# Strassen-like weight sums of three feed-forward blocks made by accumulating on-chip transfers instead of by VectorE

## The reference

```python
def swiglu(x, w_gate, w_up, w_down):
    return (jax.nn.silu(x @ w_gate) * (x @ w_up)) @ w_down
# x = x + 0.5 * swiglu(rmsnorm(x, ffn_norm), w_gate, w_up, w_down), d_model 1024, d_ff 2816
```

## Time and profile before

| | us |
|---|---|
| median of 3 runs | 2056.55 (2053.38 to 2057.03) |
| span of the profiled execution | 2054.6 |
| TensorE busy in it | 2022.2 (98%) |
| VectorE busy | 1300.4 (63%) |
| ScalarE busy | 842.5 (41%) |
| GpSimd busy | 157.6 (8%) |

### The profile page before, as it was taken

The page is one execution under the profiler, slowest core; times in us unless marked ns, Lnnn a source line. Parts: engine busy times, 40 slices in busy tenths (PEclk is TensorE's granted clock), DMA queues, the critical chain, the costliest instruction groups (busy, mean ns, idle before and its releaser), DMA issues.

```text
span 2054.6 us, 44573 instructions
## 1 busy us (share of the span) xinstructions
PE 2022.2 (98%) x18982; PEld 1924.4 (94%) x18982; DVE 1300.4 (63%) x1821; ACT 842.5 (41%) x1310; POOL 157.6 (8%) x270
## 2 busy tenths in 40 slices
PE   8999999999999999999999999999999999999999
PEld 7999999997999999999999999998566799999998
DVE  5445476778348848566785775754774438657474
ACT  5222223263334525344452442544664335435252
POOL 3002002033000000000000000000036200000000
PEclk9999999999999999999999999999999999999999
DMA  7333233201252223231423232232146632322322
GB/s 149 90 98 85 77 92 108 78 12 26 74 153 84 83 83 124 92 97 60 134 95 116 90 107 77 85 102 59 42 130 164 176 104 83 124 83 89 117 73 73
DMA packets 243917, 194.45 MB, mean 95 GB/s; under 512 B 37668, under 2 KB 221874, under 8 KB 243730
## 3 DMA queue, kind: packets, MB, share of 16 engines
q1 hardware_dynamic: 235760, 180.51, 29.2%
q0 software_dynamic: 6256, 9.23, 1.6%
q10 hardware_dynamic: 1714, 2.02, 0.4%
HBM read 184.77 MB, written 3.02 MB: 91 GB/s over the span
## 4 chain that ended last, share of the span: by engine, by line
PE 88%; DVE 6%; ACT 3%; issue 2%; DMA 0%; ACTq 0%; SPq 0%; DVEq 0%
PE ps L2382 25%; PE ps L2311 25%; PE ps L2410 24%; PE ps L2324 3%; PE ps L2824 1%; PE ps L2930 1%; PE ps L2963 1%; PE ps L3086 1%; PE ps L2724 1%; DVE stmp L657 1%; PE ps L2694 1%; PE ps L3135 1%; PE ps L3100 1%; PE ps L2907 1%; DVE xl L1551 1%
## 5 line engine op out<-in xcount | busy, mean ns | idle before, releaser
L2311 PE MATMUL ps<-xh,wh 128*128 128x260 f32 x1120 | 295.4, 285 | 2.1 <-DVE xl L1551 1.4
L2311 PE MATMUL ps<-xl,wh 128*128 128x260 f32 x1120 | 292.0, 283 | 0.0
L2410 PE MATMUL ps<-xoh,wh 128*128 128x260 f32 x992 | 281.3, 284 | 1.3 <-DVE sq L1767 1.3
L2410 PE MATMUL ps<-xoh,wl 128*128 128x260 f32 x992 | 281.0, 283 | 0.0
L2410 PE MATMUL ps<-xol,wh 128*128 128x260 f32 x992 | 280.6, 283 | 0.0
L2382 PE MATMUL ps<-xh,wh 128*128 128x260 f32 x872 | 228.8, 284 | 0.7 <-DVE wl L1600 0.7
L983 ACT ACTIVATE wh<-rw 128x1024 fp32r<-128x1024 f32 (+1 forms) x135 | 138.8, 1029 | 218.9 <-PE ps L2382 152.0
L2382 PE MATMUL ps<-xl,wh 128*128 128x260 f32 x872 | 226.9, 282 | 0.0
L2311 PE MATMUL ps<-xh,wl 128*128 128x260 f32 x1120 | 225.8, 283 | 0.0
L906 ACT ACTIVATE wh<-raw 128x1024 fp32r<-128x1024 f32 (+1 forms) x90 | 100.5, 1116 | 294.2 <-PE ps L2311 285.9
L2311 PEld LDWEIGHTS ps<-xh,wh 128*128 128x128 f32 x1120 | 211.7, 189 | 7.1 <-issue 3.9
(11 more groups left out here) (546 smaller groups left out, 4363.3 us busy)
## 6 DMA issues: line engine op xcount, KB each, us to landing
rw<-ffn_w_gate SPq DMA_DIRECT2D x33, 1024.0 KB, 5.4
rw<-ffn_w_up SPq DMA_DIRECT2D x33, 1024.0 KB, 8.3
rw<-ffn_w_down SPq DMA_DIRECT2D x12, 2048.0 KB, 7.8
raw<-ffn_w_gate SPq DMA_DIRECT2D x22, 512.0 KB, 3.9
raw<-ffn_w_up SPq DMA_DIRECT2D x22, 512.0 KB, 3.9
raw<-ffn_w_down SPq DMA_DIRECT2D x16, 704.0 KB, 4.7
rw<-ffn_w_down SPq DMA_DIRECT2D x6, 1536.0 KB, 6.6
cb<-cache_ckv SPq DMA_DIRECT2D x72, 128.0 KB, 3.9
```

Source lines behind the costliest of these rows:

```text
L2311: got = mm(ps[0:width, bank + half, 0:HALF], w[par_][:, k * width:k * width + width], src[:, k0 + k, half * HALF:half * HALF + HALF], star ...
L2410: got = mm(ps[:, bank + mat, T0], w[:, cols], src[:, j, k, :], start=first and k == 0 and m == 0 and s == 0, stop=k == 3 and m == 1, skip_ ...
```

## The change

The four sums leave VectorE's list, with `ahead` and `begins`. GpSimd gets `sums_of_weights(name)`, called once for each of the three blocks. A sum is now made of transfers between places in SBUF, one for gate and one for up each time: a plain copy of one quarter into the buffer, and once that has landed, a transfer that adds the other quarter (`accum_op=ALU.add`). The buffers no longer swap: `one` holds the first sum, `two` the second and then the fourth, which is added in place once the second has been split. Two semaphores count the landings: `m_first` (first and third sums) and `m_second` (second and fourth). ScalarE waits for these instead of `z_sum`.

```diff
-                if kind[0] == "sum" and kind[2] in (1, 2, 4, 5):
-                    act.wait_ge(z_sum, Z["sum"] + 4 * rounds(kind[1]) + {1: 1, 2: 2, 4: 3, 5: 4}[kind[2]])
+                if kind[0] == "sum" and kind[2] == 1:
+                    act.wait_ge(m_first, M_FIRST + 96 * summed(name, kind[1]) + 64)
+                elif kind[0] == "sum" and kind[2] in (2, 5):
+                    act.wait_ge(m_second, M_SECOND + 96 * summed(name, kind[1]) + (64 if kind[2] == 2 else 96))
+                elif kind[0] == "sum" and kind[2] == 4:
+                    act.wait_ge(m_first, M_FIRST + 96 * summed(name, kind[1]) + 96)
...
-                def first_sum(p):
-
-                    load_ = sv.load[sv.start[p]]
-                    dve.wait_ge(z_in[load_ % 2], Z["in"][load_ % 2] + sv.landed(load_))
-                    if rounds(p) > 0:
-                        dve.wait_ge(z_sum, Z["sum"] + 4 * rounds(p))
-                    tt(sum_buf(name, p, 0), quarter(name, p, 0, 1), quarter(name, p, 4, 1), ALU.add).then_inc(z_sum, 1)
...
-                        ahead(n0 + 3)
...
-                        fourth_sum(p)
...
+                def split(p, j):
+
+                    pool.wait_ge(z_lo, Z["lo"] + sv.start[p] + j + 1)
+
+                def first(p):
+
+                    load_ = sv.load[sv.start[p]]
+                    pool.wait_ge(z_in[load_ % 2], Z["in"][load_ % 2] + sv.landed(load_))
+                    if rounds(p) > 0:
+                        split(p - 1, 1)
+                    else:
+                        pool.wait_ge(z_lo, Z["lo"] + sv.start[p] - 2)
+                    if summed(name, p) > 0:
+                        pool.wait_ge(m_first, M_FIRST + 96 * summed(name, p))
+                    for mat in range(2):
+                        pool.dma_start(one[:, mat], quarter(name, p, 0, 1)[:, mat]).then_inc(m_first, 16)
+                    pool.wait_ge(m_first, M_FIRST + 96 * summed(name, p) + 32)
+                    for mat in range(2):
+                        pool.dma_start(one[:, mat], quarter(name, p, 4, 1)[:, mat], accum_op=ALU.add).then_inc(m_first, 16)
+
+                def second(p):
+
+                    if rounds(p) > 0:
+                        split(p - 1, 5)
+                    for mat in range(2):
+                        pool.dma_start(two[:, mat], quarter(name, p, 0, 0)[:, mat]).then_inc(m_second, 16)
+                    pool.wait_ge(m_first, M_FIRST + 96 * summed(name, p) + 64)
+                    pool.wait_ge(m_second, M_SECOND + 96 * summed(name, p) + 32)
+                    for mat in range(2):
+                        pool.dma_start(two[:, mat], one[:, mat], accum_op=ALU.add).then_inc(m_second, 16)
+
+                def third(p):
+
+                    for mat in range(2):
+                        pool.dma_start(quarter(name, p, 0, 1)[:, mat], quarter(name, p, 0, 0)[:, mat], accum_op=ALU.add).then_inc(m_first, 16)
+
+                def fourth(p):
+
+                    split(p, 2)
+                    pool.wait_ge(m_second, M_SECOND + 96 * summed(name, p) + 64)
+                    for mat in range(2):
+                        pool.dma_start(two[:, mat], quarter(name, p, 4, 0)[:, mat], accum_op=ALU.add).then_inc(m_second, 16)
+
+                first(PLAIN)
+                second(PLAIN)
+                third(PLAIN)
+                for p in range(PLAIN, NF // 2):
+                    fourth(p)
+                    if p + 1 < NF // 2:
+                        first(p + 1)
+                        second(p + 1)
+                        third(p + 1)
```

More of the change, by code:

```diff
@@ L242, in counts @@
                 "xh": 7, "xl": 7, "xf": 5, "ev": 4 * PLAIN, "ps": 2 * PLAIN, "ph": 2 * PLAIN, "hh": NF // 2, "hl": NF,
-                "sum": 4 * r, "add": 4 * r, "seed": 2 * r, "p5": 2 * r, "u2": 2 * r, "sg": 3 * r, "h": 3 * r}
+                "add": 4 * r, "seed": 2 * r, "p5": 2 * r, "u2": 2 * r, "sg": 3 * r, "h": 3 * r}
 class Chain:
@@ L438, in yoco_step @@
         s_kb = [sem("s5_taps_blocks0"), sem("s5_taps_blocks1")]
+        m_first, m_second = g_in, gf_in
+        M_FIRST, M_SECOND = 240, 16
+        SUMS_BEFORE = {"ffn01": 0, "ffn10": TOGETHER, "ffn11": 2 * TOGETHER}
         y_tr, y_sb, y_out = sem("y_tr"), sem("y_sb"), sem("y_out")
@@ L442, in yoco_step @@
         z_hi, z_lo, z_used, z_up, z_xh, z_xl, z_xf = s_u, s_z, s_w, s_y1, s_yp, s_ysp, s_ct
-        z_ev, z_ps, z_ph, z_hh, z_hl, z_sum, z_add = s_ls, s_bb, s_bp, s_sn, s_tp, s_e, s_xe
+        z_ev, z_ps, z_ph, z_hh, z_hl, z_add = s_ls, s_bb, s_bp, s_sn, s_tp, s_xe
         z_seed, z_p5, z_u2, z_sg, z_h = s_ctc, s_sb, s_wb, s_x, s_sc
-        now = {"hi": 8, "lo": 2, "used": 4, "up": 1, "xh": 8, "xl": 1, "xf": 10, "ev": 1, "ps": 1, "ph": 1, "hh": 1, "hl": 8, "sum": 11,
+        now = {"hi": 8, "lo": 2, "used": 4, "up": 1, "xh": 8, "xl": 1, "xf": 10, "ev": 1, "ps": 1, "ph": 1, "hh": 1, "hl": 8,
                "add": 8, "seed": 8, "p5": 3, "u2": 16, "sg": 16, "h": 8, "in": (IN_0, IN_0)}
@@ L501, in raw_of, with sum_buf @@
             if j in (1, 2, 5):
-                return sum_buf(name, p, {1: 0, 2: 1, 5: 0}[j])
+                return sum_buf(name, {1: 0, 2: 1, 5: 1}[j])
             k0, m0 = {0: (0, 0), 3: (4, 0), 4: (0, 1), 6: (4, 1)}[j]
             return pair[:, :, k0:k0 + 4, m0 * P:m0 * P + P]
-        def sum_buf(name, p, which):
-            return sums_at[name][(p + which) % 2].rearrange("p (a k m) -> p a k m", a=2, k=4)
+        def sum_buf(name, which):
+            return sums_at[name][which].rearrange("p (a k m) -> p a k m", a=2, k=4)
         def quarter(name, p, k0, m0):
@@ L526, in rounds, with summed @@
             return p - PLAIN
+        def summed(name, p):
+            return SUMS_BEFORE[name] + rounds(p)
         def gbuf(p):
@@ L1604, in seven @@
                 sv, Z = SEV[name], ZB[name]
-                def first_sum(p):
-                    load_ = sv.load[sv.start[p]]
-                    dve.wait_ge(z_in[load_ % 2], Z["in"][load_ % 2] + sv.landed(load_))
-                    if rounds(p) > 0:
-                        dve.wait_ge(z_sum, Z["sum"] + 4 * rounds(p))
-                    tt(sum_buf(name, p, 0), quarter(name, p, 0, 1), quarter(name, p, 4, 1), ALU.add).then_inc(z_sum, 1)
-                def second_sum(p):
-                    dve.wait_ge(z_sum, Z["sum"] + 4 * rounds(p) + 1)
-                    if rounds(p) > 0:
-                        dve.wait_ge(z_lo, Z["lo"] + sv.start[p - 1] + 6)
-                    tt(sum_buf(name, p, 1), sum_buf(name, p, 0), quarter(name, p, 0, 0), ALU.add).then_inc(z_sum, 1)
-                def third_sum(p):
-                    tt(quarter(name, p, 0, 1), quarter(name, p, 0, 1), quarter(name, p, 0, 0), ALU.add).then_inc(z_sum, 1)
-                def fourth_sum(p):
-                    dve.wait_ge(z_sum, Z["sum"] + 4 * rounds(p) + 2)
-                    dve.wait_ge(z_lo, Z["lo"] + sv.start[p] + 2)
-                    tt(sum_buf(name, p, 0), sum_buf(name, p, 1), quarter(name, p, 4, 0), ALU.add).then_inc(z_sum, 1)
                 def hidden_lo(p, c, half):
@@ L1679, in left_over @@
                     stt(g[:, 1, T0], ps[:, C_B + 1, T0], -1.0, g[:, 1, T0], ALU.mult, ALU.mult).then_inc(z_h, 1)
-                begins = {sv.start[p]: p for p in range(PLAIN + 1, NF // 2)}
-                def ahead(n):
-                    if n + 4 in begins:
-                        first_sum(begins[n + 4])
-                    if n + 3 in begins:
-                        second_sum(begins[n + 3])
                 seven_lo(name, 1)
@@ L1702, in seven @@
                                     operand_full(PREPARE[name].get(n))
-                                    if n == sv.start[PLAIN] - 4:
-                                        first_sum(PLAIN)
-                                    elif n == sv.start[PLAIN] - 2:
-                                        second_sum(PLAIN)
                                     if n > 0 or name not in NORM:
@@ L3344, in _, with sums_of_weights @@
                 out_matrices(t)
+            def sums_of_weights(name):
+                sv, Z = SEV[name], ZB[name]
+                one, two = sum_buf(name, 0), sum_buf(name, 1)
+                def split(p, j):
[40 more added lines that the diff above has]
+                        third(p + 1)
@@ L3347, in _ @@
+            sums_of_weights("ffn01")
             pool.wait_ge(k_oe, 1)
```

10 lines of the change are left out of this document (3 added, 7 removed).

## The result

| | before | after |
|---|---|---|
| median, us (lowest to highest, 6 runs each) | 2055.78 (2053.15 to 2070.69) | 2239.65 (2234.07 to 2250.30) |
| ratio, 95% interval | | 1.0875 (1.0845 to 1.0904) |
| span of the profiled execution, us | 2054.6 | 2248.5 |
| TensorE busy, us / mean granted clock | 2022.2 / 0.996 | 2095.4 / 0.956 |

The change makes the kernel 184 us slower by the medians, 194 by the two profiled spans (the profiled execution of after was the slowest of its six). The prediction was 2074 with a range of 2053 to 2160: right in direction, far too small. First the page of after: busy times, granted clock in 40 slices, the two large DMA queues (packets, MB, share of 16 engines) and the chain that ended last.

A forecast was written before the change was run, and what follows sets the result against it. TensorE, 98% busy, was taken to bound the kernel. Span 2054.6 - 2.6 (waits given back) + 20 (late sums, three blocks) = 2072 us; with the median 2 us above the span, 2074 us, range 2053 to 2160.

The forecast's parts named there:

- Where the bound lies, removal, GpSimd idle: Blocks run at TensorE's pace; removing VectorE's 108 sums (132 us) gives back 2.6 us at most; idle GpSimd covers the issuing.
- I take 1.44 us: Assumed data time of one 256 KB accumulating transfer on GpSimd's queue, from a weight load's packets of 45 ns, times 32.
- my upper bound of 2.7: Highest price for one accumulating transfer, 2.7 us: 32 pieces per DMA engine at the software queue's 84 ns a packet.
- 11.4 + 6a: Loop time from pair to pair without load sharing, a being one accumulate's price; under 20.3 us if a is below 1.5.
- Loop: 2.3 + 6.4 + 6.4 + 4.9: Dependent sums from one pair to the next in a group: 20.0 us, against 20.3 us for a pair on TensorE.
- one load sharing 2.9 us of the loop: The next pair's weight load doubles the second sum's 2.9 us of data to 5.8, making the loop 22.9 us.
- The first successor ... loss 0: Pairs 3, 5, 9, first after another in their group, have a head start: margin 0.6 us, loss 0.
- the sign that DMA is the bound: Pair 5 stalling as much as pair 7 would show the forecast wrong, with DMA as the bound.
- Slot 2: Where a late second sum shows: TensorE waits before slot 2 of pairs 6, 7 and 10, 2 to 3 us each.
- DMA as the bound: Rival, chance 0.23: accumulates at 2.7 us make the loop 33 us, time 2230; at 2.0 us, 27.4 and 2145.

The follow-up runs named there:

- plain kernel: The changed kernel with its 216 accumulating transfers made plain copies of the same shape, queue and waits: 2120.64 us, ratio 1.0306.
- light loads: The changed kernel with pair weight loads cut to one eighth and down loads to one of eight (or six) row blocks: 2167.01 us, one run.

## Why the prediction was wrong

- **Where the bound lies, removal, GpSimd idle:** right. VectorE fell by 123 us (132 forecast: its rows of 1.22 us start 1.14 us apart when back to back, and busy time counts the overlap once), and no time came back.
- **"I take 1.44 us":** the first step that failed. Measured are 2.33 us for an accumulate in 512 B pieces and 1.61 for one in 2 KB pieces; 2.33 is nearer my upper bound of 2.7, by the queue's own packet time, than the row I chose, that of a weight load's packet. The two source reads of the Trainium skill (Collectives: The Full Stack, "The bandwidth ceiling: the fold count and why AG ≠ RS ≠ AR") give half a copy's rate, stated there for collectives: 0.89 us to 1.61 is close to that for 2 KB pieces (1.8 times), but at 512 B it is 2.6 times. The packet counts above go with that (80 a copy, 144 and 528 an accumulate); that they are the reason is argued, not tested. So the direction of the rule is borne out here, and the size depends on the pieces. By the formula 11.4 + 6a, with four of the six accumulates at 2.33, two at 1.61: 11.4 + 9.3 + 3.2 = 23.9 us instead of 20.0.
- **"Loop: 2.3 + 6.4 + 6.4 + 4.9":** the second, and independent of the price. The plain kernel's loop was 26.3 to 27.9 where 15.7 to 17.2 came out. I had counted one issue at the head of a link and let the others run beside data; there GpSimd issues four transfers in a row for 3.0 us before the next landing can be waited for (the rows of that kernel), and in the changed kernel for 4.1 us from 837.30 to 841.43. I had put the third sum's data "behind" the second's: the fourth's and the first's copies stand behind them. And I had one load sharing 2.9 us of the loop, where the light loads showed it to cost 6.1 to 7.6 us, and the down load beside the last pair of each group as much, which my working did not have: 73 us of the 184 by one run.
- **The loop put together:** 20.0 us as predicted; 3.9 more by the measured prices (23.9); about 2.5 more without any load of size (25.7 to 27.2 measured), by the rows above issue time and waiting in line, not taken apart; and about 7 for the load instead of 2.9. That is the measured 33.3. The price and the load were each about 4 us too small, the issues 2.5.
- **"The first successor ... loss 0":** wrong. It rested on a margin of 0.6 us by prices of 1.44, and let the second sum's copies land 3.9 us after the split of slot 5, where the first sum's accumulates stood ahead of them (10.8 us). Every successor waited, pair 5 as well (6.3 us on TensorE), as I had named for the sign that DMA is the bound.
- **"Slot 2" as the place:** half. The first sum, which I had landing near 792 for a read near 799, was late 18 times, 136 us against the second's 121.
- **The clock:** missing. TensorE's stalls were priced at their length; each costs about 2 us more at 1.2 GHz behind it, 73 us here.
- **The rivals:** "DMA as the bound" had the mechanism and the size: a loop of 33 us, measured 33.3; 2230 us, measured 2240. It had its loop from a price alone (2.7), so its agreement is partly luck: the price was lower, and the formula's missing terms and the clock, which it had not, filled the rest. Its losses on TensorE, 177 us, were really 120, plus 73 of slower matmuls. I gave it 0.23, and cut the range at 2160, inside it: an upper bound that comes from the same queue's own packets deserved the range's upper end.

How the 184 us divide: 119 go with the adding (dearer data and longer issues), 65 remain with plain copies. Seen from TensorE, by the profiled executions, about 120 are waits and 73 slower matmuls. These are two cuts through the same time, not terms to be added. How much of the 65 is the weight loads, issue time and waiting in line was not taken apart: plain copies were not run with light loads.

## To carry to other kernels

Before work goes from a compute engine to transfers, write down for each result when the first of its transfers may start and when its last must have landed, and compare the whole chain (issues, data, completion, and a load beside it) with that. Here a chain of 11 us, 16 with a load beside it, replaced 1.22 and cost 113 to 131 us where there were 5.5 to 10.8 us of room, and nothing where another use of the two buffers gave more. Price a TensorE stall with the slower matmuls behind it, and where a price is unknown, trust the row of the queue that will do the work over one of a similar transfer elsewhere.
